# Three norms turned before their roots are known, other PSUM banks for the norms, and modulation sums split for fp32r products

## What is computed

```python
# block 1: shift, scale, gate = split(silu(c) @ mod_w + mod_b, 3)
#   h = rms(x, g) * (1 + scale) + shift ; x = x + gate * mixer(h)
#   layer 0: a gated linear recurrence (a_w_in, a_w_out)
#   layer 1: attention with forgetting (kv_w, b_w_in, b_w_out), keys from rms(x, kv_norm_g)
def second_block(x, ...):
    for layer in range(DEPTH):                       # 2
        h = rms_norm(x, norm_mix_g[layer])
        x = x + (even_mixer(h, ...) if layer % 2 == 0 else odd_mixer(h, ...))
        h = rms_norm(x, norm_ffn_g[layer])
        x = x + swiglu(h, ffn_w1[layer], ffn_w3[layer], ffn_w2[layer])
    return x

def rms_norm(x, g):
    return x * rsqrt(mean(x * x, -1) + EPS) * g

def odd_mixer(h, w_qkv, w_out):                      # q, k, v linear in h
    return stick_breaking_attention(*split(h @ w_qkv)) @ w_out

def swiglu(h, w1, w3, w2):
    return (silu(h @ w1) * (h @ w3)) @ w2
```

## Time and profile before

| What | Value |
|---|---|
| Three timed runs | 1212.64, 1214.49, 1214.70 us; median 1214.49 |
| The profiled execution, its own time | 1212.27 us |
| Its span, first to last instruction | 1210.5 us, mean granted TensorE clock 0.991 |
| Busy: PE, PEld | 1156.7 us (96%), 1039.3 (86%) |
| Busy: DVE, ACT, POOL | 828.8 (68%), 663.0 (55%), 161.3 (13%) |
| Chain that ended last, by engine | PE 82%, DVE 9%, DMA 4%, ACT 4%, issue 1% |

### The profile page before, as it was taken

The page is one execution under the profiler, slowest core; times in us unless marked ns, Lnnn a source line. Parts: engine busy times, 40 slices in busy tenths (PEclk is TensorE's granted clock), DMA queues, the critical chain, the costliest instruction groups (busy, mean ns, idle before and its releaser), DMA issues.

```text
span 1210.5 us, 19137 instructions
## 1 busy us (share of the span) xinstructions
PE 1156.7 (96%) x7413; PEld 1039.3 (86%) x7413; DVE 828.8 (68%) x1336; ACT 663.0 (55%) x1096; POOL 161.3 (13%) x196
## 2 busy tenths in 40 slices
PE   3799999999999999999998999999999999999998
PEld 3798999998799899998897688888888987888887
DVE  6868998787766754667569466666654656766664
ACT  2557623574576455675455565445554666554452
POOL 0200000063032000333015100000000452000000
PEclk9899999999999999999999999999999999999999
DMA  9986779704656865433443335655545333556552
GB/s 329 297 291 190 249 265 307 277 2 169 217 154 209 269 197 174 128 105 105 157 140 121 124 119 195 206 177 184 199 144 170 106 122 124 181 200 208 176 186 91
DMA packets 154282, 219.82 MB, mean 182 GB/s; under 512 B 5900, under 2 KB 114864, under 8 KB 154192
## 3 DMA queue, kind: packets, MB, share of 16 engines
q1 hardware_dynamic: 152880, 216.37, 54.5%
q0 software_dynamic: 1104, 2.16, 0.5%
q10 hardware_dynamic: 208, 0.06, 0.0%
HBM read 217.53 MB, written 1.05 MB: 181 GB/s over the span
## 4 chain that ended last, share of the span: by engine, by line
PE 82%; DVE 9%; DMA 4%; ACT 4%; issue 1%; POOL 0%; SPq 0%; ACTq 0%; DVEq 0%
PE ps L754 13%; PE ps L742 7%; PE ps L746 7%; PE ps L743 7%; PE ps L758 7%; PE ps L820 6%; PE ps L821 5%; PE ps L825 5%; DMA raw_weights<-in_a_w_in 3%; DVE w_lo L1821 3%; PE ps L791 2%; PE ps L793 2%; PE ps L799 2%; DVE acc L1905 2%; PE ps L725 1%; PE ps L847 1%
## 5 line engine op out<-in xcount | busy, mean ns | idle before, releaser
L1821 DVE TENSOR_TENSOR w_lo<-raw_weights,w_hi 128x1024 fp32r<-128x1024 f32 x348 | 430.6, 1249 | 194.5 <-ACT w_hi L1415 192.8
L1415 ACT ACTIVATE w_hi<-raw_weights 128x1024 fp32r<-128x1024 f32 x348 | 363.2, 1055 | 246.8 <-DMA raw_weights<-in_a_w_in 85.7
L742 PE MATMUL ps<-act_both,w_hi 128*128 128x256 f32 x960 | 238.9, 287 | 3.0 <-ACT w_hi L1415 3.0
L743 PE MATMUL ps<-act_both,w_hi 128*128 128x256 f32 x960 | 235.8, 283 | 0.0
L742 PEld LDWEIGHTS ps<-act_both,w_hi 128*128 128x128 f32 x960 | 184.2, 192 | 7.0 <-issue 5.6
L743 PEld LDWEIGHTS ps<-act_both,w_hi 128*128 128x128 f32 x960 | 184.4, 192 | 1.1 <-issue 0.7
L754 PE MATMUL ps<-act_both,w_hi 128*128 128x512 f32 x672 | 167.8, 392 | 0.0
L754 PEld LDWEIGHTS ps<-act_both,w_hi 128*128 128x128 f32 x672 | 121.8, 189 | 22.5
L746 PE MATMUL ps<-act_both,w_lo 128*128 128x256 f32 x960 | 135.5, 284 | 0.0
L746 PEld LDWEIGHTS ps<-act_both,w_lo 128*128 128x128 f32 x960 | 124.6, 193 | 0.2 <-DVE w_lo L1821 0.2
L820 PE MATMUL ps<-w_hi,act_both 128*128 128x512 f32 x296 | 118.0, 399 | 3.4 <-POOL act_both L651 3.1
(11 more groups left out here) (283 smaller groups left out, 1623.9 us busy)
## 6 DMA issues: line engine op xcount, KB each, us to landing
raw_weights<-in_ffn_w SPq DMA_DIRECT2D x66, 1024.0 KB, 5.1
raw_weights<-in_a_w_in SPq DMA_DIRECT2D x32, 1024.0 KB, 6.0
raw_weights<-in_mod_w SPq DMA_DIRECT2D x24, 1024.0 KB, 5.7
raw_weights<-in_kv_w SPq DMA_DIRECT2D x16, 1024.0 KB, 5.8
raw_weights<-in_b_w_in SPq DMA_DIRECT2D x16, 1024.0 KB, 5.8
raw_weights<-in_od_w_qkv SPq DMA_DIRECT2D x12, 1024.0 KB, 5.1
raw_weights<-in_kv_mod_w SPq DMA_DIRECT2D x8, 1024.0 KB, 5.4
raw_weights<-in_a_w_out SPq DMA_DIRECT2D x8, 1024.0 KB, 5.4
```

The costliest lines, as they stand in the source:

```text
L742: pe.matmul(dst, wh[:, k, :], act_hi[:, base + k, :], start=(k == 0), stop=False)
L743: pe.matmul(dst, wh[:, k, :], act_lo[:, base + k, :], start=False, stop=False)
L1415: act.activation(half_view(w_hi, s), HALVES[s][2], ACT.Copy).then_inc(hi_done, 1)
L1821: dve.tensor_tensor(half_view(w_lo, s), HALVES[s][2], half_view(w_hi, s).bitcast(F32), ALU.subtract).then_inc(lo_done, 1)
```

## The change

It has these parts. *Norms 3, 4 and 5* turn bare x: `pe.transpose` against the identity, each group of four as soon as the part of x is there, with no diagonal. ScalarE then computes the features' high parts after three of the four squares, and the last square, Ln and Exp after them. The root is put back at the results. For that TensorE multiplies ones by the diagonals (`root_row`, a row of 256 roots on all partitions, one for each of these norms), ScalarE copies the row to SBUF (`take_root_row`), and VectorE multiplies each gate by it (40 added multiplications in the two feed-forward stages together, and the first two gates of each stage, which ScalarE took from PSUM before, now go through VectorE's multiplication), or queries and keys as they are copied; values and the feed-forward result are multiplied by the root of the token on their partition, the latter in `add_y`. VectorE takes the queries, which ScalarE took. *Banks*: the units of norms 2, 3 and 5 move to banks 4 to 7, the first unit of keys in the first block to bank 6, the first of queries in the odd mixer to bank 4. *Norm 1*: the second copy of the features stands after all four pairs of the first. *The first low weight half* is waited for where it is used, one half at a time, and in norms 3 to 5 VectorE converts low halves ahead of the additions. *Modulation sums* 4 to 15: GpSimd splits each sum into a high and a low part, and TensorE's products of them are fp32r, with two columns where there was one.

```diff
+        UNIT_BANK = [4 + u % 4 if s in ("norm2", "norm3", "norm5") else u % 4 for u, (s, _) in enumerate(UNITS)]
+        UNIT_BANK[FIRST["k"]], UNIT_BANK[FIRST["od_q0"]] = 6, 4
...
+            def split_acc(m):
+
+                hi, lo = acc_parts(m)
+                pool.wait_ge(mod_summed, 2 * (m + 1))
+                pool.wait_ge(mod_cols, m)
+                pool.tensor_copy(hi, acc[:, m % 2, :]).then_inc(acc_hi_done, 1)
+                pool.wait_ge(acc_hi_done, m - 3)
+                pool.tensor_tensor(lo, acc[:, m % 2, :], hi.bitcast(F32), ALU.subtract).then_inc(acc_lo_done, 1)
...
-                if u >= 4:
-                    pe.wait_ge(unit_free[UNITS[u - 4][1]], before(UNITS[u - 4][1], u - 4))
+                v = unit_before(u)
+                if v is not None:
+                    pe.wait_ge(unit_free[UNITS[v][1]], before(UNITS[v][1], v))
...
                 for t in range(NT):
-                    pe.wait_ge(diag_done, 2 * j + t + 1)
-                    for k in range(KD) if t else in_bank_order:
-                        if j > 0 and t == 0 and k % 2 == 0:
-                            pe.wait_ge(x_done, 4 * (j - 1) + (first + k // 2) % 4 + 1)
+                    if j < 3:
+                        pe.wait_ge(diag_done, 2 * j + t + 1)
+                    for k in range(KD):
+                        if j >= 3 and k % 4 == 0:
+                            pe.wait_ge(x_done, 4 * (j - 1) + 2 * t + k // 4 + 1)
...
+                            ins = pe.transpose(part, chunk, ident)
...
+            def root_row(j):
+
+                pe.wait_ge(diag_done, 2 * j + 2)
+                for t in range(NT):
+                    ins = pe.matmul(row_bank(j)[:, t * P:(t + 1) * P], ones, diag[:, t, :], start=True, stop=True)
+                ins.then_inc(row_ready, 1)
...
+                    if m in (4, 5, 14, 15):
+                        pe.matmul(bank, ones_r, hi, start=True, stop=False)
+                        ins = pe.matmul(bank, ones_r, lo, start=False, stop=True)
+                    else:
+                        for c in range(4):
+                            dst = bank[:, 2 * c:2 * c + 2]
+                            pe.matmul(dst, hi[:, c * P:(c + 1) * P], ones_r[:, 0:2], start=True, stop=False)
+                            ins = pe.matmul(dst, lo[:, c * P:(c + 1) * P], ones_r[:, 0:2], start=False, stop=True)
...
+                for t, n in ((0, 0), (0, 1), (1, 0), (1, 1)):
+                    if j < 3 or t + n < 2:
+                        squares(t, n)
...
+                if j >= 3:
+                    squares(1, 1)
...
-            advance(first_half[AT[("w1", 0, 0)]] - 1)
-            add_y(2, False, first_half[AT[("w1", 0, 0)]])
+            advance(first_half[AT[("w1", 0, 0)]] + 1)
+            add_y(2, False)
...
+                        dve.tensor_tensor(gate_sum[:, d % 2, :], gate_sum[:, d % 2, :], rstd_row, ALU.mult)\
+                            .then_inc(st("gate_full"), 1)
```

More of the change, by code:

```diff
@@ L214, in build, with unit_before, row_bank @@
         ps = ctx.enter_context(nc.psum_tensor("ps", [P, 8, HALF], F32))
+        UNIT_BANK = [4 + u % 4 if s in ("norm2", "norm3", "norm5") else u % 4 for u, (s, _) in enumerate(UNITS)]
+        UNIT_BANK[FIRST["k"]], UNIT_BANK[FIRST["od_q0"]] = 6, 4
         def unit_bank(u):
-            return ps[:, u % 4, :]
+            return ps[:, UNIT_BANK[u], :]
+        def unit_before(u):
+            return next((v for v in range(u - 1, -1, -1) if UNIT_BANK[v] == UNIT_BANK[u]), None)
+        def row_bank(j):
+            return ps[:, 5 if j == 4 else 4, 0:T]
         def fox_chunk(h):
@@ L578, in split_output @@
                     .then_inc(freed, 1)
+            def split_acc(m):
[5 more added lines that the diff above has]
+                pool.tensor_tensor(lo, acc[:, m % 2, :], hi.bitcast(F32), ALU.subtract).then_inc(acc_lo_done, 1)
             outs = [0]
+            for m in range(4, 12):
+                split_acc(m)
             for i in range(HA + 2):
@@ L876, in norm @@
                 banks = [open_unit(f"norm{j}") for _ in range(4)]
[L877 removed]
                 for t in range(NT):
[L879 to L885 removed]
+                    if j < 3:
[3 more added lines that the diff above has]
+                            pe.wait_ge(x_done, 4 * (j - 1) + 2 * t + k // 4 + 1)
+                        at = (k % 2) * T + t * P
+                        part, chunk = banks[k // 2][:, at:at + P], x[:, t, k * P:(k + 1) * P]
+                        if j < 3:
+                            ins = pe.matmul(part, chunk, diag[:, t, :], start=True, stop=True)
+                        else:
+                            ins = pe.transpose(part, chunk, ident)
                         if t == NT - 1 and k % 2 == 1:
@@ L1454, in norm, with take_root_row @@
                     ins.then_inc(h_hi, 1)
-                    if j == 1 and u >= 1:
-                        self_features(u - 1)
                 if j == 1:
-                    self_features(3)
+                    for u in range(4):
+                        self_features(u)
+                if j >= 3:
+                    squares(1, 1)
+            def take_root_row(j):
+                act.wait_ge(row_ready, j - 2)
+                act.activation(rstd_row, row_bank(j), ACT.Copy).then_inc(row_copied, 1)
             def self_features(u):
```

145 lines of the change are left out of this document (93 added, 52 removed).

## The result

The changed kernel took 1206.52 us (median of five runs, 1202.86 to 1208.06) against 1214.08 us for the kernel before (median of five); the ratio is 0.995, with a 95% interval of 0.9933 to 0.9968. A second series of five gave 1207.81 us and a ratio of 0.9962 (0.995 to 0.9973). Each ratio is to the kernel before, timed in the same series. The forecast was 1202 us, a ratio of 0.990. The direction is right and 1206.52 lies in the range of 1197 to 1208, but the gain is about half of what was forecast: 4 to 8 us by the intervals of the ratios instead of 12. The profiled execution took 1202.86 us, the fastest of its five, with a span of 1201.0 us.

What follows compares the result with a forecast made beforehand. TensorE, busy 96% of 1210.5 us, was taken as the bound, with time won at its stops. Norms 10.8 us plus modulation sums 0.8 made 11.6 off, about 1202 us after adjusting to the timed runs; range 1197 to 1208.

Steps and rivals of the forecast that it cites:

- Norms 3, 4 and 5, norm 2, the root rows: Earlier first products gain 3.25, 3.0, 4.05 and 0.75 us; three root rows cost TensorE 1.35 in all.
- Norm 1: gain 1.15, not 2: First keys' product starts about 2 us earlier, but the next high weight half limits the gain to 1.15 us.
- rival A: At the norms: TensorE's clock falls to half, costing 1.7 us each, 5.1 at three norms, giving 1207; chance 0.12.
- In the attention ... 0 again, at most 0.75 each: Attention between feed-forward stages: three query copies moved from ScalarE to VectorE cost 0, at most 0.75 us each.
- VectorE's low halves ahead of the additions at norm 5: Norm 5: VectorE's low halves fit into its idle time ahead of the additions; norm 5 gains 4.05 us.
- Modulation sums, forecast 0.8: Split sums gain 1.7 us at gates and columns and 0.9 at the last columns, lose 1.8 in the first projection.
- TensorE's stop near 205: First projection: TensorE's stop for a high weight half grows from 1.8 us to about 3.
- Feed-forward multiplications at 0: Feed-forward stages: forty added VectorE multiplications of about 0.42 us cost 0, at the other end 1 us a layer.
- Final scaling, 0.06: End of the kernel: scaling the result by the root costs about 0.06 us more.
- B: First projection: each of eight splits delays the chain by 0.88 us, with a longer low clock, giving 1209; chance 0.06.
- C: Feed-forward: multiplications hold the gate path, 20 iterations lose 0.84 us each, 17 in all, giving 1219; chance 0.04.
- D: At the norms: L725 waits for something other than the bank; half the norms' gain is left, 1207; chance 0.05.

Runs made afterwards that it cites:

- e12: The changed kernel with the first two gate units of both feed-forward stages back in the banks of the norm's first two units; 1214.7 us, ratio 1.0026.
- e14: The changed kernel with norm 1 as before: second copy of the features between the pairs, keys' first unit in its old bank; 1205.79 us, ratio 0.9944.
- e6: The changed kernel without the multiplications of 36 gates by the root's row (timing only, results wrong); 1207.69 us, ratio 0.996.
- e15: The kernel before, with VectorE copying the attention's outputs before it takes the next keys in the odd mixer; 1210.74 us, ratio 0.9988.
- e5: The changed kernel with gates from the third on multiplied by the root's row twice (timing only, results wrong); 1208.13 us, ratio 0.9967.
- e8: The changed kernel with attention outputs copied before queries and keys in the odd mixer, and norm 5's low halves behind the additions; 1201.91 us, ratio 0.9921.
- e4: The changed kernel with VectorE making the first two low weight halves at norm 5 behind the four additions, not ahead; 1203.64 us, ratio 0.9936.

## Why the forecast gave too large a gain

The steps that failed are the terms that priced moved and added work at nothing or too favourably: two of VectorE's takes in the odd mixer, put at 0, lost 1.43 us; VectorE's low halves ahead of norm 5, said to fit into idle time, lost 1.96; the modulation sums, put at a gain of 0.8, lost 0.5; and norm 1, put at a gain of 1.15, gave 0. Against the forecast that is 5.8 us; the other norms gave 0.4 more than forecast, which leaves 5.4, the distance from 11.6 to the 6.2 below.

*Norms 3, 4 and 5, norm 2, the root rows* (forecast 9.7 us with the roots): right, 10.1 by the trace, and for the reason given. Each chain was followed to the engine that is late next, and it was ScalarE each time; e12 confirms the bank. The price of a shared bank was put too low.

*"Norm 1: gain 1.15, not 2"*: wrong. The step read 338.50 as the end of the old order's chain and took the half clock from 331.65 as part of the background. ScalarE's weight half at 336.25, which the step itself names as unmoved, would have fed L742 near 337.4 in the old order too. The row of the granted clock was used for rival A and not for this place. It measured 0 (e14).

*"In the attention ... 0 again, at most 0.75 each"*: the bound was the truth for two of three, 1.43 us. The reason given, that TensorE waits for nothing of VectorE's there, was false: the trace had two waits of 0.6 us for VectorE's copies behind the take of the keys. A third and fourth of the same kind were the nearest row, and I did not take it.

*VectorE's low halves ahead of the additions at norm 5*: I wrote that they "fit into its idle time". They fit into VectorE's, and not into GpSimd's: 1.96 us lost. The step asked who waits for the moved instruction, but not who shares the port while it runs.

*Modulation sums, forecast 0.8*: the gates as said (0.74 for 0.8); the columns 0 for 0.45 each, the lower bound, where the trace has eight loads of weights and eight passes as before (that the loads set the pace is not shown); the splits' cost 1.2 for 1.8. In sum 0.5 lost instead of 0.8 won. TensorE's stop near 205, forecast to grow from 1.8 to about 3, grew from 2.09 to 2.37 from start to start.

*Feed-forward multiplications at 0*: right (e6). *Final scaling, 0.06*: not separately seen.

The change's own sum by the traces is 10.1 - 1.4 - 2.0 + 0.7 - 1.2 = 6.2 us, and the two series measured 4.6 and 6.1 by their ratios. I can't say more exactly how much of the rest the clock took: a fall behind norm 1 costs 1.5 us in five of twelve traces, and the fall near 209 us is in two of three traces of the kernel before (the third is e15) and in three of thirteen of changed ones, too few for a rate. Rival A had the mechanism: at norm 3 the clock fell in two of twelve traces (e5, e8, about 1.5 us each where the rival had 1.7), at norm 5 in none, not at three norms each time. B, C and D did not come. The range, 1197 to 1208, held the median by 1.5 us; with four terms wrong that is luck, since its upper part was there for rivals A and B, which hardly came.

## What to carry to other kernels

Before an instruction is moved into an engine's idle time, look at which other engine works in that time on the same ports, and whether that one is waited for. Where a trace has already one stop of a kind, a second instruction of the same kind at the same place gives a second one. Read the clock's row at every place where a gain is booked: a stage that ran at half clock under a wait looks like one that is late for its order.

## What the hardware showed that I had not expected

A GpSimd copy of 128x256 took 1.45 us instead of 0.40 beside a VectorE subtraction with two SBUF inputs, and a subtraction 1.58 instead of 0.74, while VectorE lost 0.2 (2.56 us for two conversions, 2.36 in e4). An fp32r product with two columns costs as much as an fp32 pass with one, 0.11 us from start to start in both. And two stops of TensorE, lengthened from 2.0 and 0.9 us to 4.5 and 3.3, cost 7.8 us by the trace, 3.0 of them because the clock fell to 0.50 behind each.
